# A two-layer encoder trunk on one core: roots of the grouped outputs by logarithm and exponential, spread one step later, and adaLN work dealt out anew

## What is computed

```python
def encoder_layer(x, mod, ...):
    shift_a, scale_a, gate_a, shift_f, scale_f, gate_f = jnp.split(mod[:, None, :], N_MOD, axis=-1)
    h = rms_norm(x, g_attn) * (1.0 + scale_a) + shift_a
    proj = h @ w_in                      # q_a, k_a, v_a, c_q, c_kv, k_r
    ...
    o_a = block_attention(q_a, k_a, v_a)          # 8 heads, 2 kv heads, head_dim 64
    ...
    o_b = block_attention(q_full, k_full, v_b)    # 8 latent heads
    o = jnp.concatenate([rms_norm(o_a, g_out_a), rms_norm(o_b, g_out_b)], axis=-1) @ w_o
    x = x + gate_a * o
    h = rms_norm(x, g_ffn) * (1.0 + scale_f) + shift_f
    u = depthwise_conv_centred(h @ w_up, conv_w, conv_b)
    val, gate = jnp.split(u, 2, axis=-1)
    return x + gate_f * ((jax.nn.silu(gate) * val) @ w_down)

def encode(x, c, w_ada, b_ada, ...):
    c_act = jax.nn.silu(c)
    for l in range(2):
        mod = c_act @ w_ada[l] + b_ada[l]         # "adaLN": 6 vectors of 1024 per layer
        x = encoder_layer(x, mod, ...)
    return rms_norm(x, g_final)
```

## Time and profile before

| | |
|---|---|
| median of 3 runs | 1223.06 us (1219.8 to 1224.69) |
| the profiled execution, its time | 1222.51 us |
| its span, first to last instruction | 1220.7 us |
| mean granted clock of TensorE | 0.971 |
| TensorE busy | 1162.3 us (95%) |
| VectorE, ScalarE, GpSimd busy | 751.4, 511.6, 571.4 us |
| DMA | 151.68 MB, mean 124 GB/s |

### The profile page before, as it was taken

How to read it: one execution, slowest core, us unless ns; L and a number is a source line. 1 busy time by engine, 2 the same in 40 slices (tenths; PEclk the granted TensorE clock), 3 DMA queues, 4 the chain that set the end, 5 groups by cost and what they waited for, 6 DMA issues and landing times.

```text
span 1220.7 us, 18778 instructions
## 1 busy us (share of the span) xinstructions
PE 1162.3 (95%) x6264; PEld 963.0 (79%) x6264; DVE 751.4 (62%) x1507; ACT 511.6 (42%) x922; POOL 571.4 (47%) x783
## 2 busy tenths in 40 slices
PE   9999988899979999899999999799999999999997
PEld 6896666798868888688788966589988888888886
DVE  6887655767786687657856577656676134412345
ACT  5436663254421334224345367634443233423442
POOL 2562331654554455544556425235464645554462
PEclk8999988999989999899999999899999999999998
DMA  9844500324455444553433201013242223222222
GB/s 350 313 157 151 213 18 18 139 73 140 167 189 181 147 161 161 177 190 138 172 104 104 104 35 35 18 35 104 82 168 96 104 86 103 93 99 85 103 86 70
DMA packets 44123, 151.68 MB, mean 124 GB/s; under 512 B 5138, under 2 KB 7954, under 8 KB 44052
## 3 DMA queue, kind: packets, MB, share of 16 engines
q1 hardware_dynamic: 44052, 150.77, 34.6%
HBM read 148.65 MB, written 2.10 MB: 123 GB/s over the span
## 4 chain that ended last, share of the span: by engine, by line
issue 34%; PE 32%; POOL 20%; POOLq 10%; DVE 2%; DMA 1%; DVEq 0%; ACT 0%; SPq 0%; ACTq 0%
POOL w_lo L600 19%; PE ps L687 11%; PE ps L693 10%; PE ps L688 10%; POOLq L602 7%; POOLq L660 2%; POOLq L658 1%; DVE ada_prod L1708 1%; PE ps L819 1%; DMA ada_raw<-ada_slots 1%; PE ps L707 0%; DVE x L1641 0%; POOLq L613 0%; DVE h_lo L1751 0%; DVE mod L1716 0%
## 5 line engine op out<-in xcount | busy, mean ns | idle before, releaser
L600 POOL TENSOR_TENSOR w_lo<-w_raw,w_hi 128x256 fp32r<-128x256 f32 x712 | 530.8, 777 | 504.9 <-ACT w_hi L1243 470.7
L687 PE MATMUL ps<-h_hi,w_hi 128*128 128x512 f32 (+1 forms) x864 | 316.8, 367 | 2.0 <-POOLq L603 1.9
L688 PE MATMUL ps<-h_lo,w_hi 128*128 128x512 f32 (+1 forms) x864 | 316.0, 366 | 0.0
L693 PE MATMUL ps<-h_hi,w_lo 128*128 128x512 f32 (+1 forms) x864 | 315.9, 366 | 0.0
L1243 ACT CAST w_hi<-w_raw 128x1024 fp32r<-128x1024 f32 x178 | 183.1, 1047 | 194.7 <-PE ps L687 194.1
L2006 DVE SCALAR_TENSOR_TENSOR u_sb<-ps,par,u_sb 128x510 f32<-128x510 f32 x176 | 131.8, 749 | 118.5 <-ACT u_sb L1447 104.2
L687 PEld LDWEIGHTS ps<-h_hi,w_hi 128*128 128x128 f32 x864 | 163.3, 189 | 29.3 <-POOLq L603 2.7
L688 PEld LDWEIGHTS ps<-h_lo,w_hi 128*128 128x128 f32 x864 | 163.3, 189 | 26.1
L693 PEld LDWEIGHTS ps<-h_hi,w_lo 128*128 128x128 f32 x864 | 163.2, 189 | 26.0
L687 PE MATMUL ps<-a_hi,w_hi 128*128 128x512 f32 (+1 forms) x400 | 150.2, 376 | 17.8 <-DVEq L1695 12.1
L1525 DVE SCALAR_TENSOR_TENSOR ada_prod<-ada_raw,ps 128x512 f32<-128x512 f32 x224 | 144.9, 684 | 8.0
(11 more groups left out here) (182 smaller groups left out, 1500.7 us busy)
## 6 DMA issues: line engine op xcount, KB each, us to landing
w_raw<-w_slots SPq DMA_DIRECT2D x178, 512.0 KB, 3.5
ada_raw<-ada_slots SPq DMA_DIRECT2D x88, 512.0 KB, 4.1
shift<-shift_slots SPq DMA_DIRECT2D x8, 512.0 KB, 13.3
x_tok<-x_rows SPq DMA_DIRECT2D x4, 512.0 KB, 9.7
x<-x_t SPq DMA_DIRECT2D x4, 512.0 KB, 14.0
y_t<-x SPq DMA_DIRECT2D x3, 512.0 KB, 2.9
y_t<-x SPq DMA_DIRECT2D x1, 256.0 KB, 2.9
y_t<-x SPq DMA_DIRECT2D x2, 128.0 KB, 2.7
```

The lines of the kernel that those rows point to most:

```text
L600: nc.gpsimd.tensor_tensor(w_lo[:, j, c], w_raw[:, j, c], w_hi[:, j, c].bitcast(F32), ALU.subtract)
L687: hh = mm(out, stat[0], mov[0], start=first, stop=False)
L688: hl = mm(out, stat[0], mov[1], start=False, stop=False)
L693: return mm(out, stat[1], mov[0], start=False, stop=last)
```

## The change

The group's root becomes `exp(-0.5 * ln(sum/512 + eps))`, two activations on ScalarE with a drain between them, and VectorE's reciprocal goes away with its semaphore; TensorE's spread waits for ScalarE. A table set that holds both functions is loaded once ahead of the loop, and the load for the square root moves behind the last high part. Group 0's root is taken in step 12 ahead of that step's exponentials, where it stood behind them. Its spread moves from the end of step 12 to step 13, between fill and transposes. The scalings, high parts and low parts of events 0 to 3 are dealt out one or two a step, with two of the low parts after the loop. In steps with both, outputs go ahead of the streamed products.

The plan takes fewer adaLN slots at the ends of the feed-forward groups of layer 0 (30 in place of 34, of which group 0 has 11 for 12, group 1 12 for 13, group 2 7 for 9) and four in layer 1's input stage. Vector 9, which these are part of, is taken full width. The four slots of layer 0's output projection are taken as eight half slots, one sequence each, over seven tiles.

```diff
-HALVED = (4, 5, 6, 7, 8, 9, 10)
+HALVED = (4, 5, 6, 7, 8, 10)
...
-    ups = [[1, 2, 1, 2, 1, 2, 1, 2], [2, 2, 1, 2, 1, 2, 1, 2], [2, 2, 2, 2, 1, 0]]
+    ups = [[2, 1, 2, 1, 2, 1, 1, 1], [2, 2, 1, 2, 1, 2, 1, 1], [2, 2, 1, 1, 1, 0]]
...
+    plan += [((1, "in", n), SLOTS + at, takes) for n, at, takes in ((1, 6, 2), (2, S_UQ, 1), (3, S_UQ, 1))]
...
-                    pe.wait_ge(group_inverted, 3 * L + n + 1)
+                    pe.wait_ge(group_root, 3 * L + n + 1)
...
+                    if i == NA + 5:
+                        group_spread(0)
...
+                    if 0 <= i - 3:
+                        outputs(i - 3) if i < NP + 2 else None
                     if L == 0 and 0 <= i - 1 < 4 * len(STREAMED):
                         stream_products(i - 1)
-                    if 0 <= i - 3:
-                        outputs(i - 3) if i < NP + 2 else None
                     if i == NA + 3:
                         group_sums(0)
-                    if i == NA + 4:
-                        group_spread(0)
...
-                A(st_o[:, 1, GROUP_AT[n] + tiles[0]:GROUP_AT[n] + tiles[-1] + 1], ps[:, SUM_BANK[n], tiles[0]:tiles[-1] + 1], ACT.Sqrt,
-                  bias=eps[:], scale=1.0 / 512).then_inc(group_root, 1)
+                A(st_o[:, 1, at], ps[:, SUM_BANK[n], tiles[0]:tiles[-1] + 1], ACT.Ln, bias=eps[:], scale=1.0 / 512)
+                nc.scalar.drain()
+                A(st_o[:, 0, at], st_o[:, 1, at], ACT.Exp, scale=-0.5).then_inc(group_root, 1)
...
-                prepare(ACT.Exp)
+                nc.scalar.preload_act_table_set("natural_log_exp_and_others")
...
+                    if i == NA + 4:
+                        group_roots(L, 0)
                     if i < NP:
                         act.wait_ge(max_ready, NP * L + i + 1)
...
-                    if i == NA + 4:
-                        group_roots(L, 0)
-                    if NA + 6 <= i < NA + 10:
-                        output_hi(L, i - NA - 6)
+                    if i in (NP - 2, NP - 1):
+                        output_hi(L, i - NP + 2)
                     if i == NP:
-                        prepare(ACT.Sqrt)
+                        output_hi(L, 2)
+                        output_hi(L, 3)
...
+                prepare(ACT.Sqrt)
...
+            def ada_halves(L, parts):
+
+                if L > 0:
+                    return
+                for _ in range(parts):
+                    n, j = DVE_SLOTS[taken[0]]
+                    ada_part(n, j, half_taken[0])
+                    taken[0] += half_taken[0]
+                    half_taken[0] = 1 - half_taken[0]
...
                 for e in range(TAIL, KD):
                     update(e)
                     add_square(n, e - 1)
+                    between(e)
...
-                    if i == NA + 4:
-                        group_inverse(L, 0)
-                    if i == NA + 5:
-                        output_scaled(L, 0)
-                        output_scaled(L, 1)
-                    if i == NA + 6:
-                        output_scaled(L, 2)
-                    if i == NA + 7:
+                    if NA + 5 <= i < NP:
+                        output_scaled(L, i - NA - 5)
+                    if i == NP - 1:
+                        output_scaled(L, 3)
                         output_lo(L, 0)
-                        output_scaled(L, 3)
                     if i == NP:
                         output_lo(L, 1)
-                        output_lo(L, 2)
                 take_outputs(NP - 2)
+                output_lo(L, 2)
                 output_lo(L, 3)
...
-                norm(2 * L + 1, lambda m: ("wo", m), lambda i: ("wo_half", i), GATE_A, lambda m: ada_at(L, ("wo", m)))
+                norm(2 * L + 1, lambda m: ("wo", m), lambda i: ("wo_half", i), GATE_A, lambda m: ada_halves(L, (1, 1, 1, 2, 1, 1, 1, 0)[m]))
```

More of the change, by code:

```diff
@@ L454, in encoder_kernel @@
         group_root = sem("group_root")
-        group_inverted = sem("group_inverted")
         group_full = sem("group_full")
@@ L1253, in group_roots @@
                 tiles = GROUP_TILES[n]
-                A(st_o[:, 1, GROUP_AT[n] + tiles[0]:GROUP_AT[n] + tiles[-1] + 1], ps[:, SUM_BANK[n], tiles[0]:tiles[-1] + 1], ACT.Sqrt,
-                  bias=eps[:], scale=1.0 / 512).then_inc(group_root, 1)
+                at = slice(GROUP_AT[n] + tiles[0], GROUP_AT[n] + tiles[-1] + 1)
+                A(st_o[:, 1, at], ps[:, SUM_BANK[n], tiles[0]:tiles[-1] + 1], ACT.Ln, bias=eps[:], scale=1.0 / 512)
+                nc.scalar.drain()
+                A(st_o[:, 0, at], st_o[:, 1, at], ACT.Exp, scale=-0.5).then_inc(group_root, 1)
             def output_hi(L, e):
@@ L1505, in ada_slot @@
                     ada_part(n, j, s)
+            half_taken = [0]
+            def ada_halves(L, parts):
[6 more added lines that the diff above has]
+                    half_taken[0] = 1 - half_taken[0]
             c_half = [None]
@@ L1642, in final @@
                                            op0=ALU.mult, op1=ALU.mult).then_inc(y_done, 1)
-            def group_inverse(L, n):
-                dve.wait_ge(group_root, 3 * L + n + 1)
-                tiles = slice(GROUP_AT[n] + GROUP_TILES[n][0], GROUP_AT[n] + GROUP_TILES[n][-1] + 1)
-                V.reciprocal(st_o[:, 0, tiles], st_o[:, 1, tiles]).then_inc(group_inverted, 1)
             def output_scaled(L, e):
@@ L1959, in _ @@
                         pad_c()
-                    if i == NA + 4:
-                        group_inverse(L, 0)
-                    if i == NA + 5:
-                        output_scaled(L, 0)
-                        output_scaled(L, 1)
-                    if i == NA + 6:
-                        output_scaled(L, 2)
-                    if i == NA + 7:
+                    if NA + 5 <= i < NP:
+                        output_scaled(L, i - NA - 5)
+                    if i == NP - 1:
+                        output_scaled(L, 3)
                         output_lo(L, 0)
-                        output_scaled(L, 3)
                     if i == NP:
                         output_lo(L, 1)
-                        output_lo(L, 2)
                 take_outputs(NP - 2)
+                output_lo(L, 2)
                 output_lo(L, 3)
-                group_inverse(L, 1)
                 for e in range(KD // 2, KD):
@@ L1980, in _ @@
                     output_lo(L, e)
-                group_inverse(L, 2)
                 for e in range(KD, N_EVENTS):
```

## The result

The changed kernel takes **1191.45 us** (median of 4 runs, 1189.9 to 1192.63) against 1223.88 us for the kernel before (4 runs): a ratio of 0.9739, 95% interval 0.9711 to 0.9768, so some 32 us less. The forecast was 1195.5 us. The profiled execution of the changed kernel took 1192.63 us, with a span of 1190.8 us and a mean granted clock of 0.989.

A forecast was written before the change was run, and what follows sets the result against it. TensorE was taken as the bound, busy 1162.3 of 1220.7 us, gains coming from its waits and low-clock stretches. Terms summed to 27.1 us off 1222.5, forecast 1195.5; 1189 to 1202 at 0.55, full range 1184 to 1210.

The forecast's parts named there:

- Attention up to the last row scaling: Attention's group stage: stretch between outputs 6.4 us shorter in layer 0, 5.5 in layer 1; a later wait 0.4 shorter each.
- the streamed order: Layer 0's attention, steps 4 to 6: outputs ahead of streamed products fill three waits of 0.44; 1.3 us, 0 to 2.
- three steps: Attention's group stage: root on a shared table, root ahead of exponentials, spread a step later; priced within 6.4 and 5.5 us.
- The tail: End of attention: TensorE waits for low parts, clock likely falls; between 0.7 us better and 2.5 worse.
- The halves of the output projection: Layer 0's output projection: a wait of about 4.9 us replaces two of 2.1; -0.5 us, -2.5 to +3.
- The feed-forward groups: Layer 0: fewer adaLN takes before the last tiles shorten waits; 4.0, 5.3 and 6.9 us in groups 0, 1, 2.
- Layer 1's input stage: Four adaLN slots moved here as full-width sums, covered by input projection and latent work: 0 us, -1.5 at worst.
- VectorE as the bound: Rival, chance 0.20: low parts and late sums hand waits on, each followed by a clock fall; 13.4 us less, 1209.
- the table not shared: Rival, chance 0.05: logarithm and exponential load their own tables at each attention group; 9 us less gain, 1204.
- no change: Rival, chance 0.02: gains of the attention loop lost in the tail and again in the norm.
- The clean case: Rival, chance 0.15: shortened waits are too short for the clock to fall; 36.5 us less, 1186.
- The slower rival: Rival, chance 0.03: full-width sums starve GpSimd's splits in group 2 and layer 1's input stage; 1230 us.

The follow-up runs named there:

- the kernel with three edits: Changed kernel with low parts of events 2 and 1 ahead of VectorE's copies, and adaLN takes moved earlier in groups 0 and 1: 1180.52 us.
- the plan's own kernel: Kernel before with only the new adaLN plan of the feed-forward groups: 1206.51 us, ratio 0.9854.
- its own experiment: Changed kernel with every adaLN sum full-width, none halved: 1200.4 us, ratio 0.9824.

## Why the prediction was right, and where its terms were off

**Attention up to the last row scaling: right.** Forecast 6.4 + 0.4 in layer 0 and 5.5 + 0.4 in layer 1, with the streamed order's 1.3 on top: 8.1 and 5.9. The cut gives 9.56 and 6.27. From outputs to outputs 4.91 was measured where 4.96 was forecast, and the wait before the transposes of step 14 is 0.77, forecast 0.75. The mis-sized term is the streamed order, 2.7 and not 1.3: I counted the wait of 0.44 and not what a product gains that follows other work at once. What the prediction lacked is that its three steps cover each other: it named the delay of each and not that two of them would have done.

**The tail: right in kind.** Forecast waits 0.4, 2.3, 1.8, 0.4; measured 0.38, 1.96, 1.88, none. The low parts took 1.15 to 1.21 each, but 0.68 for the first; the rows of the kernel with three edits say why. I gave the tail a loss of 1.3 (between 0.7 better and 2.5 worse). From the transposes of step 14 to the first product behind the last outputs are 15.06 us, 14.94 before: no loss, no gain. One move of a line showed that the order I had followed through was the limit itself.

**The halves of the output projection: wrong in its step, small in its sum.** I put VectorE's chain at 241.3 at the first sum of squares. It ended at 235.8 (the row at 234.82), which is 241.0 in the time of the kernel before (the products of the projection start 5.2 earlier): right. I put TensorE there at 236.4, "without its two waits and the fall of the clock". That failed: it still waited 0.71 and 2.07 for splits, and the clock fell (the window at 225.5). Spreading the sums doesn't free the splits: beside one or two sums of a tile GpSimd's four quarters still took 4.25 and 4.89 us, and TensorE's waits end within 0.2 of their ends. Both engines arrive together, and the wait of 4.9 that I forecast does not exist. Measured gain 1.1 from the first product to the feed-forward part (51.96 to 50.84), 0.8 by the kernel with whole slots; forecast -0.5.

**The feed-forward groups: right, a little low.** The third down tiles wait 1.76 and 1.52 where I wrote 2.0 to 2.4, and no clock fell behind them, where I had left half of the fall. Whether it falls in group 0 hung on little: among the nine profiles with such a wait it fell in the five with 1.83 to 2.02 us and not in the four with 1.76 to 1.81. Group 2's two waits are gone from their places, and 0.41 at its third down tile and 0.83 for a split stand later (about 0.6 each was said). Not foreseen: the split wait of 1.30 at 288.94, from the two slots behind the first up tile. In sum 19.1 (forecast 16.2), and 16.7 in the plan's own kernel, where the fall behind the first third tile stayed.

**Layer 1's input stage: no cost, as said.** TensorE waits nowhere for 0.15 us or more between 624 and 698. What was not foreseen is the fall behind the last norm of layer 0, 1.84 us. The wait ahead of it is 1.69 long in both kernels (in the changed one at 623.98); in the kernel before, the clock stayed up.

**The rivals.** VectorE as the bound (1209), the table not shared (1204), and no change are out by the time; no table load stands in the loop. The clean case (1186) isn't reached, since the falls of the two tails and of the projection stayed. The kernel with low part 2 first has its time, 1186.1, but not its condition: the clock still fell in layer 1's tail. The slower rival is out by its own experiment. What is left of the forecast's error: 33.7 us from the start of attention against 27.1, in the streamed order 1.4, tails and group stages 2.5, halves 1.6, feed-forward 2.9, less 1.8 for the last norm, together 6.6; less what the start-up of the profiled execution took, 4.3 in this one. The Trainium skill, "ScalarE: Activation LUTs", section "What ACT_TABLE_LOAD costs", would have made the two removed loads worth 2.7 us each; two loads put back cost under a microsecond in each layer, so there neither that nor 1.28 each lay on the path in full.

**Two readings of the kernel before that were off,** though no term hangs on them. GpSimd isn't on half of the chain that ended last: the page gives it 30%, 20% at work and 10% in its queue. And VectorE isn't without idle time in the feed-forward groups: in each up tile it waits some 0.8 us twice for ScalarE (0.82 at 276.48 and 0.81 at 277.98), inside the chain that the prediction counted.

## What to carry to other kernels

When several late things stand in one chain, price them together and then ask what each costs with the others gone: here undoing one of three steps costs 0.5 to 0.8 us, and together they took 5.6 out of layer 1's group stage. After a hand-made order has been followed through on paper and two waits for the same engine remain, look at once for work of that engine with no early reader ahead of them, as the copy of pair 14 here: one moved line was worth 2.3 us in layer 0's tail, and two gave 3.3 and 3.6 in the two tails. And a resource that contends is a loss only where its idle time ends: 87 us more of split work cost 9.

## What was not expected of the hardware

**The same waits, and different falls of the clock.** In the tails of the kernels with the changed kernel's order (waits of 0.38, 1.96 and 1.88), the stretch from the transposes of step 14 to the third of these waits' products took 10.5 us in ten of eighteen and 11.6 to 13.3 in the others, with the clock at 0.50 for some 3.5 us or for longer, nearly 14 in one of them (0.51 from 778 to 792 in the kernel with the attention parts alone). Behind the third down tile of group 0 nearly equal waits, 1.81 and 1.83 in two of the kernels, came without a fall and with one; a fall there makes the next 130 us 1.6 longer. The last norm of layer 0, with the same wait of 1.7 in all, was followed by a fall of 1.8 in four of fourteen profiles. These are the few microseconds by which kernels of one order differ, and they were more than the effects of most single steps. The cuts of the time line, stretch by stretch, separate the two; the times don't.

**The start-up.** Attention began between 110.4 and 114.8 us in the profiles, 112.0 and 114.8 for one and the same program. The early one had the clock at 0.74 in its first 20 us and the late one at 1.00 (windows of the changed kernel's second and first execution):

```profile
0.00:20.00 20.00, 18.93 (x82) 11.76 (x82) 9.56 (x18) 12.06 (x18) 5.21 (x10) 0.74 0.85 315
```

```profile
0.00:20.00 20.00, 18.93 (x64) 11.50 (x68) 8.73 (x16) 11.02 (x16) 3.13 (x8) 1.00 0.86 314
```

The early execution did more by then (82 matmul rows against 64) in spite of the lower clock. The same split runs through all fourteen profiles: the eight with 0.74 or 0.83 in this window have 80 to 87 rows and start attention between 110.4 and 112.4, the six with 1.00 have 64 rows and start between 112.4 and 114.9. What sets this is open; no kernel was made for it.
